# The gates of the modulation: weighed and folded on GpSimd in the ring slots, one matmul by ones each, made just ahead of their use

## The reference, cut to what matters

```python
c_act = jax.nn.silu(c)
for l in range(DEPTH):
    mod = c_act @ w_ada[l] + b_ada[l]
    sh_m, sc_m, gt_m, sh_f, sc_f, gt_f = jnp.split(mod[:, None, :], N_MOD, axis=-1)
    h = rms_norm(x, g_pre_mix[l]) * (1.0 + sc_m) + sh_m
    y = token_mixer(h, w_in[l], g_moba_out[l], g_dsa_out[l], w_out[l], cos, sin)
    x = x + gt_m * rms_norm(y, g_post_mix[l])
    h = rms_norm(x, g_pre_ffn[l]) * (1.0 + sc_f) + sh_f
    y = conv_glu_ffn(h, w_up_act[l], w_up_lin[l], w_conv[l], b_conv[l], w_down[l])
    x = x + gt_f * rms_norm(y, g_post_ffn[l])
```

## Time and profile before

| | us |
|---|---|
| median of 3 runs | 2486.71 (2483.31 to 2487.22) |
| profiled execution | 2486.55 |
| its span, first to last instruction | 2484.0 |
| PE busy | 2376.0 |
| DVE busy | 1721.4 |
| ACT busy | 1232.5 |
| GpSimd busy | 647.8 |

### The profile page before, as it was taken

The page is one execution under the profiler, slowest core; times in us unless marked ns, Lnnn a source line. Parts: engine busy times, 40 slices in busy tenths (PEclk is TensorE's granted clock), DMA queues, the critical chain, the costliest instruction groups (busy, mean ns, idle before and its releaser), DMA issues. The chain is left out here.

```text
span 2484.0 us, 38204 instructions
## 1 busy us (share of the span) xinstructions
PE 2376.0 (96%) x15277; PEld 1961.5 (79%) x15277; DVE 1721.4 (69%) x2003; ACT 1232.5 (50%) x1317; POOL 647.8 (26%) x347
## 2 busy tenths in 40 slices
PE   6999999899899998999988899999999999999997
PEld 4875999786799875899977478888888888888775
DVE  2565677474876775765587587878787878787576
ACT  2334543443544133333313376777767676767452
POOL 0000000000950261960063223232323232323113
PEclk9999999899999999999999899999999999999999
DMA  9897765457785585695533298999999999999672
GB/s 337 267 349 251 253 215 174 145 186 253 256 260 175 170 271 181 227 268 173 171 106 115 86 364 311 363 353 363 351 364 351 362 353 363 350 363 351 237 273 109
DMA packets 416671, 650.07 MB, mean 262 GB/s; under 512 B 37052, under 2 KB 255256, under 8 KB 416536
## 3 DMA queue, kind: packets, MB, share of 16 engines
q1 hardware_dynamic: 389328, 633.13, 73.6%
q10 hardware_dynamic: 27206, 15.03, 2.3%
HBM read 647.06 MB, written 1.05 MB: 261 GB/s over the span
## 5 line engine op out<-in xcount | busy, mean ns | idle before, releaser
L1602 ACT ACTIVATE region_part<-ring 128x2048 fp32r<-128x2048 f32 x412 | 770.0, 1908 | 272.7 <-PE bank L889 191.3
L2631 DVE TENSOR_TENSOR ring_part<-ring,region_part 128x2048 fp32r<-128x2048 f32 x240 | 569.8, 2403 | 48.9 <-PE bank L1223 23.0
L889 PE MATMUL bank<-ring_part,region_part 128*128 128x512 f32 x1480 | 578.8, 391 | 0.0
L887 PE MATMUL bank<-region_part 128*128 128x512 f32 x1288 | 512.2, 398 | 5.1 <-DVE region L2676 2.2
L888 PE MATMUL bank<-region_part 128*128 128x512 f32 x1152 | 449.4, 390 | 0.0
L1502 POOL TENSOR_TENSOR ring_part<-ring,region_part 128x2048 fp32r<-128x2048 f32 x48 | 248.2, 5178 | 509.7 <-ACT region_part L1602 423.1
L887 PE MATMUL bank<-xn_part,region_part 128*128 128x256 f32 x1152 | 326.8, 284 | 12.1 <-DVE hT_part L2232 10.2
L889 PEld LDWEIGHTS bank<-ring_part,region_part 128*128 128x128 f32 x1480 | 278.2, 188 | 60.1
L889 PE MATMUL bank<-hT_part,region_part 128*128 128x256 f32 x1152 | 324.7, 282 | 0.0
L888 PE MATMUL bank<-xn_part,ring_part 128*128 128x256 f32 x1152 | 324.5, 282 | 0.0
L2187 DVE TENSOR_TENSOR ring_part<-ring,region_part 128x2048 fp32r<-128x2048 f32 x72 | 175.7, 2449 | 177.7 <-ACT region_part L1602 177.7
(11 more groups left out here) (386 smaller groups left out, 3922.2 us busy)
## 6 DMA issues: line engine op xcount, KB each, us to landing
ring<-in_moe_w_gate SPq DMA_DIRECT2D x112, 1024.0 KB, 5.0
ring<-in_moe_w_up SPq DMA_DIRECT2D x112, 1024.0 KB, 5.1
ring<-in_moe_w_down SPq DMA_DIRECT2D x112, 1024.0 KB, 4.9
ring<-in_w_ada SPq DMA_DIRECT2D x48, 1024.0 KB, 9.5
ring<-in_mod_w SPq DMA_DIRECT2D x48, 1024.0 KB, 7.2
ring<-in_w_in SPq DMA_DIRECT2D x44, 1024.0 KB, 5.7
ring<-in_w_up_act SPq DMA_DIRECT2D x22, 1024.0 KB, 5.3
ring<-in_w_up_lin SPq DMA_DIRECT2D x22, 1024.0 KB, 5.6
```

Source lines behind the costliest of these rows:

```text
L887: nc.tensor.matmul(o, split(a_hi), split(b_hi), start=start, stop=False, skip_group_check=True)
L889: return nc.tensor.matmul(o, split(a_hi), split(b_lo), start=False, stop=stop, skip_group_check=True)
L1602: return nc.scalar.activation(out_, in_, func, **kw).then_inc(*done(*event))
L2631: v.tensor_tensor(split(w), w, whole(hi), ALU.subtract).then_inc(*done("moe_lo", j, e))
```

## The change

GpSimd takes 28 of the 32 gate chunks. `gate_part` waits for the load, multiplies the slot in place by `c_act` (each of the 8 blocks by its column, broadcast) and folds the 8 blocks to one by three additions. `gate_rows` on PE multiplies the remaining 128x256 by a matrix of ones, which sums over the partitions and leaves the gate in all of them. The picks and halves for these gates go; only the FFN gate of layer 3 (q = 20 to 23) keeps the old way. The gate chunks also move: each gate is loaded and made shortly before its use, in projections 4 to 10 (`GATE_IN`) and in the FFN's groups (`GATE_FFN`). The other sums move with them: layer 0's FFN columns to eight places, the rest of the next layer's to the first groups, and `mod_columns` from group 6 to group 2 or 3. In the projections one bank is kept for the gates.

```diff
-ADA_FIRST = {3: (8,), 4: (9,), 5: (10,), 6: (11,), 7: (12,), 8: (13,), 9: (14, 15), 10: (16,), 11: (17, 18), 12: (19,), 13: (20, 21),
-             14: (22, 23)}
+ADA_FIRST = {3: (12,), 5: (13,), 7: (14,), 9: (15,), 11: (16,), 12: (17,), 13: (18,), 14: (19,)}
+GATE_QS = (8, 9, 10, 11, 20, 21, 22, 23)
+GATE_IN = {0: {4: (0, 8), 6: (0, 9), 8: (0, 10), 10: (0, 11)}, 1: {4: (1, 20), 6: (1, 21), 8: (1, 22), 10: (1, 23)}}
+GATE_FFN = {0: {3: (0, 20), 4: (0, 21), 5: (0, 22), 6: (0, 23), 7: (1, 8), 8: (1, 9), 9: (1, 10), 10: (1, 11)},
+            1: {4: (2, 8), 6: (2, 9), 8: (2, 10), 10: (2, 11)},
+            2: {6: (2, 20), 7: (2, 21), 8: (2, 22), 9: (2, 23), 10: (3, 8), 11: (3, 9), 12: (3, 10), 13: (3, 11)}}
+COLUMNS_AT = (2, 2, 3)
-S5_ADA = {8: (0,), 1: (1,), 2: (2, 3), 3: (4,), 6: (5,), 7: (6, 7), 4: (8, 9, 10, 11)}
+S5_ADA = {8: (0,), 1: (1,), 2: (2,), 3: (3,), 6: (4,), 7: (5,), 4: (6, 7)}
...
-    q = ADA_MIX + ADA_PASS + g
-    return [q] if q < ADA else []
+    if l == 2:
+        return [18 + 2 * g, 19 + 2 * g] if g < 3 else []
+    return [18 + g] if g < 2 else []
...
+def gate_place(q):
+
+    return 2 * (q >= 20) + q % 4 // 2, q % 2
+
+
+def gate_used(l, q):
+
+    h, j = gate_place(q)
+    return ("pe_tile", "gate", l, h) if j else ("pe_used", "ada", l, q)
...
+                if i in GATE_IN[l]:
+                    plan.append((("ada", *GATE_IN[l][i]), gate_used(*GATE_IN[l][i])))
...
             if g:
                 plan.append((("down", l, 0, g - 1), chunk_used(("down", l, 0, g - 1))))
+            if g in GATE_FFN[l]:
+                plan.append((("ada", *GATE_FFN[l][g]), gate_used(*GATE_FFN[l][g])))
...
+            def gate_rows(l, q, among):
+
+                h, j = gate_place(q)
+                if j == 0:
+                    bank(("gate", l, h), ("mod_gate", l, h), among)
+                pe.wait_ge(*until("pool_chain", "gate", l, q, 1))
+                m = nc.tensor.matmul(psum[bank_of["gate", l, h]][:, j * CW:(j + 1) * CW], ones, chunk(("ada", l, q))[:, 0, :],
+                                     start=True, stop=True)
+                m.then_inc(*(done("pe_tile", "gate", l, h) if j else done("pe_used", "ada", l, q)))
...
-                    ada_sum(l + 1, "mix", u, 0)
+                    if u not in GATE_QS:
+                        ada_sum(l + 1, "mix", u, 0)
                     if l == 0 and u == 1:
                         mod_columns(0, 1, range(5))
-                        gate_half(0, 0, range(5))
-                        gate_half(0, 1, range(5))
-                    if l == 0 and u == 5:
-                        gate_half(0, 2, range(5))
-                        gate_half(0, 3, range(5))
...
-                    if g == 6:
+                    if g == COLUMNS_AT[l]:
                         mod_columns(l + 1, "rest", (3,))
-                    if 7 <= g < 11:
-                        gate_half(l + 1, g - 7, (3,))
+                    if l == 2 and g in (4, 5):
+                        gate_half(3, g - 2, (3,))
...
                     if 0 < g < groups - 1:
                         down(g - 1)
+                    if g in GATE_FFN[l]:
+                        gate_rows(*GATE_FFN[l][g], (3,))
...
+                    usable[0] = range(6 + l)
...
+                        if i - 1 in GATE_IN[l]:
+                            gate_rows(*GATE_IN[l][i - 1], (6 + l,))
...
+            def gate_part(l, q):
+
+                w = chunk(("ada", l, q))
+                pool.wait_ge(*loaded(("ada", l, q)))
+                by = c_act[:, l // 2, :].unsqueeze(2).broadcast_to([P, KD, CW])
+                nc.gpsimd.tensor_tensor(w, w, by, ALU.mult).then_inc(*done("pool_chain", "gate", l, q, KD))
+                for k in (4, 2, 1):
+                    pool.wait_ge(*done.prev())
+                    nc.gpsimd.tensor_tensor(w[:, 0:k, :], w[:, 0:k, :], w[:, k:2 * k, :], ALU.add)\
+                        .then_inc(*done("pool_chain", "gate", l, q, k))
...
                 for g in range(ffn_groups(l)):
                     if g == 0 and l == 2:
                         gains(l, "mix")
+                    if g in GATE_FFN[l]:
+                        gate_part(*GATE_FFN[l][g])
                     for k, h0 in steps[:4 if g == 0 else 1]:
                         table_step(l + 1, k, h0)
...
-                            gate_out(0, 0)
-                            gate_out(0, 1)
-                            pick_gate(0, 2)
-                            pick_gate(0, 3)
-                        if l == 0 and u == 5:
-                            gate_out(0, 2)
-                            gate_out(0, 3)
...
-                    if g == 5:
-                        acc_out(l + 1, "rest", ADA - 1)
...
+                    if g == COLUMNS_AT[l] - 1:
+                        acc_out(l + 1, "rest", last_ada(l + 1))
...
+                    if l == 2 and g in (4, 5):
+                        gate_out(3, g - 2)
+                    if g in GATE_FFN[l] and GATE_FFN[l][g][1] % 2:
+                        gate_out(GATE_FFN[l][g][0], gate_place(GATE_FFN[l][g][1])[0])
...
+                        if i in (8, 12):
+                            gate_out(l, 2 * l + (i == 12))
```

More of the change, by code:

```diff
@@ L245, in chunk_plan @@
                         plan.append((("ada", 0, q), ("pe_used", "ada", 0, q)))
+                if i in GATE_IN[l]:
+                    plan.append((("ada", *GATE_IN[l][i]), gate_used(*GATE_IN[l][i])))
             for q in range(ADA_MIX):
-                plan.append((("ada", l + 1, q), ("pe_used", "ada", l + 1, q)))
+                if q not in GATE_QS:
+                    plan.append((("ada", l + 1, q), ("pe_used", "ada", l + 1, q)))
         else:
@@ L1477, in ffn @@
                     table_start(l + 1)
-                if l == 0:
-                    return
-                steps = list(TABLE_STEPS)
+                steps = list(TABLE_STEPS) if l else []
                 for g in range(ffn_groups(l)):
@@ L1565, in _ @@
                 if l < 2:
+                    if l == 0:
+                        pool.wait_ge(*until("c_raw"))
+                    for q in GATE_IN[l].values():
+                        gate_part(*q)
                     for g in range(2):
@@ L2140, in pick_gate @@
             def pick_gate(l, h):
-                if h >= 2:
-                    dve.wait_ge(*until("pe_tile", "gate", l, h - 2))
                 for j in range(2):
@@ L3136, in _ @@
                     if l == 0:
[L3137 to L3139 removed]
+                        acc_out(0, 1, last_ada(0))
                     after()
```

18 lines of the change are left out of this document (7 added, 11 removed).

## The result

| | before | changed kernel |
|---|---|---|
| median of the runs, us | 2486.59 (2483.31 to 2487.22, 4 runs) | 2534.78 (2531.81 to 2538.70, 4 runs) |
| ratio to before, 95% interval | | 1.020 (1.0186 to 1.0213) |
| profiled execution, span, us | 2484.0 | 2536.8 |

What follows compares the result with a forecast made beforehand. PE was taken to bound the kernel. From 2486.55 us, stage terms summing to -20.1 plus 1 for the folds gave 2467.5, stated as 2468; forecast 2463 to 2472 (0.62), 8 in 10 range 2460 to 2478.

Steps and rivals of the forecast that it cites:

- What bounds the kernel: Whole kernel: PE is busy 2376.0 of 2484.0 us, so work taken from it shortens the program where PE is full.
- The sum of -20.1: PE's time stage by stage, layer 0's projections to FFN 2: gains and losses add to -20.1 us; layer 3 and mixture unchanged.
- PE's prices and the chain of the fold: PE: lone sum 1.20 us, matmul by ones 0.45 to 0.50; GpSimd: one chunk's fold some 9.3 us, fitting before its matmul.
- PE waits for the fold: Rival: load and fold exceed 25.2 us, PE stands still at each matmul by ones; 2491 to 2507 us, chance 0.06.
- the slots: Ring slots: in layer 0's projections gate chunks hold theirs one projection longer, costed at nothing; the rival has the slot behind late.
- I charge 1 us for all folds: Shared SBUF ports: 28 GpSimd folds holding back DVE's subtractions cost PE 1 us in all, nothing at the low end.
- DVE's 36.2 us of idle time: FFN 0: DVE was idle 36.2 us before its 21 subtractions, made a group ahead; used to argue for the small charge.
- The filled window of FFN 1: 627 to 720 us: GpSimd busy 91.1 of 93, PE still 88.2; a group with a fold has half that GpSimd density.
- ports: Rival: folds hold back DVE's subtractions so PE waits, 0.2 to 0.5 us per fold; 2472 to 2481 us, chance 0.18.
- move nothing: DVE's gate additions wait for PE's down products; the next group's subtractions behind them wait for the same, so nothing moves.
- The signs: Expected rows: 32-column sums 1536 to 1088, 56 matmuls by ones, layer 0's projections shrink 6 to 7 us, exponential waits some 8.
- The alarm: Forecast wrong if PE's waits name GpSimd's additions or DVE's subtractions with over 5 us, among other conditions.

Runs made afterwards that it cites:

- e1: Changed kernel with the folds of its 28 gate chunks left out; GpSimd multiplies one column of each and signals. Measured 2466.07 us.
- e2: Changed kernel with each whole fold cut into 15 GpSimd operations over 128x256 (8 products, 7 additions). Measured 2499.85 us.
- e4: Changed kernel with the product made as 8 single-input operations over 128x256 with a column as factor; additions as they were. Measured 2519.19 us.
- e5: Changed kernel with DVE's gate additions in the FFNs moved ahead of S5's parameters and columns of their group. Measured 2533.77 us.
- e3: Changed kernel without the three additions of each fold; the product stays in one piece. Measured 2497.99 us.
- e11: As e10, but the gate chunk of group 4 stays in group 4 of FFN 0. Measured 2487.07 us.
- e8: Changed kernel with ACT making the products, a column as scale, and GpSimd only 7 additions over 128x256 per fold. Measured 2491.33 us.
- e10: Changed kernel with ACT's products in layer 0's projections, FFN 0 and FFN 2, GpSimd's pieces elsewhere, FFN 0's group 4 gate chunk in group 2. Measured 2488.02 us.

## Why the prediction was wrong, by its own steps

- **What bounds the kernel: right.** Taking 20 us of work from PE gave 19 to 22 us (e1: 19.2 by the medians, 22.0 by the spans).
- **The sum of -20.1: right, nearly term by term.** In e1 layer 0's projections shrank by 6.0 (6.5 foreseen), attention 0 by 3.9 (3.7), FFN 0 with the norms around it by 3.8 (4.2), layer 1's mixer grew by 1.8 (0.7), FFN 1 shrank by 7.2 (6.2), layer 2's mixer by 1.9 (1.5), FFN 2 grew by 0.2 (1.3). Attention 1 gave nothing of its 1.3.
- **PE's prices and the chain of the fold: right.** 9.7 us for a fold (9.3; the product is shorter than the 4.65 charged, and the additions, held by DVE in their turn, longer), PE's wait for GpSimd's additions 2.4 us in all. The rival "PE waits for the fold" and the slots were the wrong place to look for a slower result, and so the 0.06 for "slower" stood on a mechanism that didn't occur.
- **"I charge 1 us for all folds": the step that failed.** It measured 69 us. Two parts of its argument were wrong. It weighed the ports against DVE's long subtractions alone, where a meeting costs at most a GpSimd operation for 2.3 us of work (35 of the 143 us that DVE is held); a row of short operations pays it again and again: 2.75 us of work became 9.15. And it took DVE's 36.2 us of idle time before the subtractions for slack. Idle time ahead of an instruction says when its input came, not how late its output may be. The filled window of FFN 1 was no cover for these folds either. GpSimd's operations in it were short ones of 1.27 us; with e2's pieces of 0.6 to 0.7 us FFN 1 lost 0.8 us, with the changed kernel's operations of up to 3.6 us it lost 7.4.
- **The rival "ports"** had the mechanism, a chance of 0.18, and a price of 0.2 to 0.5 us for each fold; 2.5 were measured. The rule of the Trainium skill that stood beside it (SBUF — State Buffer, "SBUF: two separate sides") is what the rows show for GpSimd operations with two tensor inputs: an exclusive hold for the whole instruction. It should have been worked out with the shortest DVE operations, not the longest. By the Trainium skill (the same page, "Who interferes with whom") a DVE operation with one input counts only in a two-port mode, and it names casts and `tensor_scalar` among those that can be in one. The trace agrees: TENSOR_SCALAR over 128x16 (0.54 for 0.17 in e2) and CAST over 128x256 (844 ns for 387) were held too, while operations that read PSUM kept their times (0.68 for the gate addition at 366.25). One thing differs: beside GpSimd's products with one tensor input the hold was not for the whole instruction (e4: 0.42 us, twice in 0.9).
- **DVE's gate additions "move nothing": right** in effect for the changed kernel (e5), though PE's wait of 3.67 us for the bank was real.
- **The signs.** The sums fell to 1088 matmuls and by 29 us, 56 records by ones came, the waits for exponentials rose to 10.5 us (8 foreseen). Layer 0's projections grew by 6.5 us where they should have shrunk. The alarm that was set off is the one named: DVE's subtractions in PE's waits with more than 5 us. Those of the weights have 13.4, those of x and of the hidden activations 16.8 and 23.0.

## What to carry to other kernels

Before giving GpSimd elementwise work over SBUF, look in DVE's timeline for chains of small operations in the stretch where it will run, and price each of them at the length of one GpSimd operation; DVE's busy share doesn't show them. If such work must go to GpSimd, cut it to operations about as short as DVE's (here half the loss went with no other change, though the fold got longer and came late once), give a part to ACT, and put it only in stages where an experiment shows DVE with room. Leaving the new work out, with all its order and signals kept, is the cheapest first experiment: it split the result at once into -20 and +69.

## What the runs showed of the hardware

- A product with a broadcast column (128x2048, f32) takes GpSimd 3.6 us, the subtraction of two tensors of that size 4.65. With one tensor input and a column as scalar, 256 columns take 0.92 us undisturbed, twice as long per column (1.35 on average beside DVE), but hold DVE for a part of the time only.
- After the stall of 11.4 us PE's matmuls started 0.21 us apart in place of 0.12 for 4.6 us, from 122.0 to 126.6, and after the stall of 7.0 us for 4.0 us, from 375.2 to 379.2. So a stall in such a stretch costs some 2 us more than itself.
- With the sums gone from attention 0, the granted clock there was 0.61 to 0.69 in e2, e3 and e11 (windows from 186 or 180 us on) and 1.00 in e1, e8 and e10, whose matmuls there are the same. From the transposes of attention 0 to w_out e2 took 49.2 us, and e3, e4 and e11 50.8, where e1 took 44.1, so 5 to 7 us of the profiled runs of e2 and e3 are no direct price of the folds. What decides between the two wasn't found; in the kernel before, with the sums in place, the clock was 1.00 from 180 to 205 us.
